# Matrix memory in a two-model transformer kernel: the guard and reciprocal of a token tile's two heads taken in one pass

## The reference

```python
def mlstm_scan(q, k, v, log_i, log_f, state):          # one direction
    ...
        b = jnp.cumsum(fc, axis=-1)
        d_intra = jnp.where(causal, b[..., :, None] - b[..., None, :] + ic[..., None, :], -jnp.inf)
        ...
        w_intra = jnp.exp(d_intra - m_t[..., None])
        s = jnp.einsum('bhtd,bhsd->bhts', qc, kc) * w_intra
        num = w_prev[..., None] * (q C) + jnp.einsum('bhts,bhse->bhte', s, vc)
        qn = w_prev * (q n) + jnp.sum(s, axis=-1)
        h = num / jnp.maximum(jnp.abs(qn), jnp.exp(-m_t))[..., None]

def mlstm_group(...):
    hx_f, hc_f = direction(False, ...)                 # forward
    hx_b, hc_b = direction(True, ...)                  # backward
    y = head_layernorm(hx_f + hx_b, norm_g) * sigmoid(o)
```

## Time and profile before

| | |
|---|---|
| median of 3 runs | 3306.86 us (3305.32 to 3307.8) |
| the profiled execution, own time | 3306.95 us |
| its span | 3305.0 us |
| PE busy | 98% of the span |
| DVE busy | 56% |
| ACT busy | 19% |
| mean granted clock of PE | 0.996 |
| `pairs` of layer 2 | from about 2111.7 to 2325 us |
| `pairs` of layer 3 | from about 2884.6 to 3048 us |

### The profile page before, as it was taken

One profiled execution on the slowest core, in us unless ns is written; L12 is line 12 of the kernel. 1 busy time (PEld: TensorE's weight loads), 2 busy tenths in 40 slices (PEclk: granted clock), 3 DMA queues, 4 the chain that ended last, 5 costly groups with the idle time before them and its releaser, 6 DMA issues.

```text
span 3305.0 us, 40572 instructions
## 1 busy us (share of the span) xinstructions
PE 3224.5 (98%) x15270; PEld 2430.0 (74%) x15270; DVE 1864.2 (56%) x3731; ACT 638.6 (19%) x1339; POOL 160.6 (5%) x307
## 2 busy tenths in 40 slices
PE   7999999999999999999999999999999999999999
PEld 5888865548888878888667886444488887456888
DVE  5887842638887788778353613355274775254100
ACT  2000023421000020000342002355210001254100
POOL 0000000000000000000000100000000000000000
PEclk9999999999999999999999999999999999999999
DMA  7554522114554345544224855211142332331553
GB/s 268 164 175 149 173 70 71 42 49 163 169 169 155 115 153 166 167 153 133 94 80 160 284 155 162 64 52 58 47 158 90 129 120 77 123 101 40 166 152 102
DMA packets 115186, 422.72 MB, mean 128 GB/s; under 512 B 13040, under 2 KB 16368, under 8 KB 112976
## 3 DMA queue, kind: packets, MB, share of 16 engines
q1 hardware_dynamic: 75232, 265.32, 25.0%
q0 software_dynamic: 39504, 154.77, 14.6%
q10 hardware_dynamic: 288, 0.36, 0.0%
HBM read 418.29 MB, written 1.31 MB: 127 GB/s over the span
## 4 chain that ended last, share of the span: by engine, by line
PE 93%; DVE 3%; ACT 2%; issue 1%; DMA 1%; DVEq 0%; ACTq 0%; SPq 0%
PE PS L917 30%; PE PS L969 18%; PE PS L862 11%; PE PS L1423 6%; PE PS L1025 6%; PE PS L1403 3%; PE PS L1347 2%; PE PS L990 2%; PE PS L1265 2%; PE PS L1096 1%; PE PS L1487 1%; PE PS L1203 1%; PE PS L766 1%; PE PS L757 1%; PE PS L1057 1%
## 5 line engine op out<-in xcount | busy, mean ns | idle before, releaser
L862 PE MATMUL PS<-xn,ring 128*128 128x256 f32 (+1 forms) x1504 | 372.0, 408 | 2.8 <-ACT xn L1690 2.3
L862 PEld LDWEIGHTS PS<-xn,ring 128*128 128x128 f32 x1504 | 283.9, 190 | 89.0 <-issue 45.9
L917 PE MATMUL PS<-xn,ring 128*128 128x256 f32 x1312 | 301.4, 383 | 3.7 <-ACT xn L1681 3.7
L917 PEld LDWEIGHTS PS<-xn,ring 128*128 128x128 f32 x1312 | 246.8, 191 | 56.4 <-issue 19.1
L1423 PE MATMUL PS<-xn,arena 128*128 128x512 f32 (+1 forms) x640 | 256.5, 534 | 1.4 <-ACT arena L1913 1.4
L969 PE MATMUL PS<-xn,ring 128*128 128x256 f32 x752 | 223.7, 379 | 0.0
L2202 DVE SCALAR_TENSOR_TENSOR mix<-arena,cond,mix 128x1024 f32<-128x1024 f32 x182 | 222.6, 1278 | 0.0
L969 PE MATMUL PS<-arena,ring 128*128 128x256 f32 x784 | 202.1, 380 | 0.3
L969 PE MATMUL PS<-xn 128*128 128x256 f32 x752 | 193.0, 379 | 0.0
L1025 PE MATMUL PS<-arena,ring 128*128 (+1 forms) x864 | 186.8, 379 | 0.0
L1025 PEld LDWEIGHTS PS<-arena,ring 128*128 128x128 f32 x864 | 164.2, 190 | 22.3
(11 more groups left out here) (327 smaller groups left out, 4892.3 us busy)
## 6 DMA issues: line engine op xcount, KB each, us to landing
ring<-stream SPq DMA_DIRECT2D x500, 512.0 KB, 3.7
arena<-fed_w POOLq DMA_DIRECT2D x200, 512.0 KB, 4.0
arena<-pair_m POOLq DMA_DIRECT2D x8, 1536.0 KB, 7.1
mix<-fed_w POOLq DMA_DIRECT2D x24, 512.0 KB, 3.9
arena<-pair_n POOLq DMA_DIRECT2D x8, 1024.0 KB, 5.4
mix<-gate_sums POOLq DMA_DIRECT2D x32, 256.0 KB, 4.4
mix<-na_bias POOLq DMA_DIRECT2D x8, 512.0 KB, 4.0
h<-xT SPq DMA_DIRECT2D x1, 1024.0 KB, 6.6
```

The costliest lines, as they stand in the source:

```text
L862: m = pe.matmul(PS[:, bank, 0:tokens], ring[:, s, k * P:(k + 1) * P], xn[:, k, 0:tokens], start=k == 0, stop=k == DC - 1)
L917: m = pe.matmul(out, weights, moving, start=k == 0, stop=k == 3)
```

## The change

`weighted(i, n)`, one head of a tile, becomes `weighted(i, t)`, both heads. The four row sums of a tile (two heads by two directions) go to four columns of `small`; maximum, guard and reciprocal are taken once on the four columns instead of twice on two; then come the two scalings of head 0 and the two of head 1. The waits for the weights and scores of head 1 now stand ahead of that one pass. The engines other than DVE are untouched.

```diff
-                def weighted(i, n):
-                    t, e = n // 2, n % 2
-                    w = (wt0, qkn)[e]
-                    dve.wait_ge(pm_w, i * per + (N0 + n + 1))
-                    dve.wait_ge(pm_score, i * per + (N0 + n + 1))
+                def weighted(i, t):
+                    full, less = 1 - t % 2, t % 2
                     spans = (SPAN[t], BOTH[t]) if t % 2 else (BOTH[t], SPAN[t])
-                    for d in range(2):
-                        cols = spans[d]
-                        ins = dve.tensor_tensor_reduce(w[:, d, cols], PS[:, pm_bank(n), cols], w[:, d, cols],
-                                                       1.0, 0.0, ALU.mult, ALU.add, small[:, d:d + 1])
+                    for e in range(2):
+                        n = 2 * t + e
+                        w = (wt0, qkn)[e]
+                        dve.wait_ge(pm_w, i * per + (N0 + n + 1))
+                        dve.wait_ge(pm_score, i * per + (N0 + n + 1))
+                        for d in range(2):
+                            cols = spans[d]
+                            ins = dve.tensor_tensor_reduce(w[:, d, cols], PS[:, pm_bank(n), cols], w[:, d, cols], 1.0,
+                                                           0.0, ALU.mult, ALU.add, small[:, 2 * d + e:2 * d + e + 1])
                     link(ins)
-                    link(stt(small[:, 2:4], small[:, 0:2], -1.0, small[:, 0:2], ALU.mult, ALU.max))
-                    link(tt(small[:, 2:4], small[:, 2:4],
-                            gcol[:, t, 1, :, bass.ds(i * 2 + e, 1)].rearrange("p d o -> p (d o)"), ALU.max))
-                    link(dve.reciprocal(small[:, 4:6], small[:, 2:4]))
-                    if n >= 2:
-                        dve.wait_ge(pm_turned, i * per + (N0 + n - 1))
-                    full, less = 1 - t % 2, t % 2
-                    link(dve.tensor_scalar(probs[:, e, SPAN[t]], w[:, full, SPAN[t]], small[:, 4 + full:5 + full], None,
-                                           ALU.mult))
-                    stt(probs[:, e, BOTH[t]], w[:, less, BOTH[t]], small[:, 4 + less:5 + less], probs[:, e, BOTH[t]],
-                        ALU.mult, ALU.add).then_inc(pm_p, 1)
-                    dve.wait_ge(pm_p, i * per + (N0 + n + 1))
+                    link(stt(small[:, 4:8], small[:, 0:4], -1.0, small[:, 0:4], ALU.mult, ALU.max))
+                    guards = gcol[:, t, 1, :, bass.ds(i * 2, 2)]
+                    lower = small[:, 4:8].rearrange("p (d e) -> p d e", e=2)
+                    link(tt(lower, lower, guards, ALU.max))
+                    link(dve.reciprocal(small[:, 8:12], small[:, 4:8]))
+                    for e in range(2):
+                        n = 2 * t + e
+                        w = (wt0, qkn)[e]
+                        if n >= 2:
+                            dve.wait_ge(pm_turned, i * per + (N0 + n - 1))
+                        scale = lambda d: small[:, 8 + 2 * d + e:9 + 2 * d + e]
+                        link(dve.tensor_scalar(probs[:, e, SPAN[t]], w[:, full, SPAN[t]], scale(full), None, ALU.mult))
+                        stt(probs[:, e, BOTH[t]], w[:, less, BOTH[t]], scale(less), probs[:, e, BOTH[t]],
+                            ALU.mult, ALU.add).then_inc(pm_p, 1)
+                    dve.wait_ge(pm_p, i * per + (N0 + 2 * t + 2))
...
-                    for n in range(per):
-                        weighted(i, n)
+                    for t in range(tiles):
+                        weighted(i, t)
```

More of the change, by code:

```diff
@@ L2706, in pairs @@
                 with dve.Fori(0, HP - 1) as i:
-                    start = loop(i, 7 + 5 * per + tiles)
+                    start = loop(i, 7 + 3 * per + tiles)
                     iteration(i, False)
```

## The result

The changed kernel takes 3369.79 us (median of 4 runs, 3368.08 to 3371.23) against 3307.33 us (4 runs): a ratio of 1.0188, with a 95% interval of 1.0173 to 1.0203. That is 62.5 us slower. The forecast was 3359 us, in a range of 3339 to 3377.

The account below looks back on a forecast made before the run. PE, busy 98% of the span, was taken to bound the kernel. New waits of 38 us plus 14 us of clock gave 52 us on 3306.95, so 3359 us, range 3339 to 3377.

Parts of the forecast that it names:

- Reading where PE waits: PE's waits in L1487 for L2652, 18 times, 18.9 us, are all that a faster DVE could give back.
- What is removed: DVE, 24 tiles of layers 2 and 3: one maximum, guard and reciprocal pass less per tile, 0.71 us each, 17 us.
- Head 0 waits for head 1: Layer 2, tile 0, iterations 2 to 4: head 0's scalings wait for head 1's reductions; PE's first transpose 3.96 us late.
- The chain through ACT in later tiles: Layer 2, tiles 1 to 3: even transposes wait for copy, head 1's weights and DVE; new waits 1.96, 1.07, 1.16 us.
- Sum of the waits: New waits of PE in both layers cost 38 us: 21.7 in layer 2, 16.6 in layer 3.
- The clock: Layers 2 and 3: PE's granted clock falls to 0.50 at long waits, costing 14 us, with 5 and 24 as ends.
- The second: Clock falls after nearly all 16 waits and slow transposes stretch the chain through ACT: above 3374 us; chance 0.1.
- the first: Waits as forecast, but clock falls few or hidden: 38 to 43 us, 3345 to 3350 us; chance 0.2.
- The third: DVE's saving reaches PE: at most all 18.9 us of waits go, 3288, more likely half, 3297 us; chance 0.03.
- The fourth: PE's matmuls cover the later transposes, so no change; chance 0.04.

Follow-up runs that it names:

- the wait alone: Kernel before, steps unmerged, but DVE waits for head 1's weights and scores between head 0's reductions and small steps: 3340.53 us, ratio 1.0102.
- earlier weights: Changed kernel, ACT making head 1's weights for the next iteration's tile 0 before its inverse-sums wait and sigmoid: 3342.15 us, ratio 1.0107.
- run without tile 0: Changed kernel with the merged pass in all tiles but tile 0, which takes its heads one by one as before: 3338.64 us, ratio 1.0092.
- the run with filled waits: Changed kernel with matmuls nobody reads put on PE ahead of each wait for an even transpose: 3345.69 us, ratio 1.0118.
- the run without the guard: Kernel before without L2644, the maximum with exp(-m), so it no longer computes the function: 3300.81 us against 3306.50, ratio 0.9985.
- tile 0 alone: Changed kernel with the merged pass in tile 0 only, other tiles taking heads one by one as before: 3329.19 us, ratio 1.0068.
- the order without the merge: Changed kernel's order, but maximum, guard and reciprocal in two passes of two columns: 3388.62 us, ratio 1.0248.

## Why the prediction was right, point by point

- **Reading where PE waits.** Right: the only line that mattered was L1487 for L2652, and no other line in these stages of the changed trace has new waits.
- **What is removed.** DVE's busy time fell by 13.4 us; 17 was the start-to-start time with its gaps. Four columns cost 0.16, 0.16 and 0.18 us, as taken.
- **Head 0 waits for head 1.** Shown by two runs and the trace: the wait alone costs 34 us, earlier weights give 27.6 back, and DVE's idle 2.76 us for L1988 stands in the rows. The 3.13 us that the forecast put behind the start of head 1 contain the other part, head 1's reductions ahead of head 0's scalings. For T0 3.13 us after the start of head 1 were forecast and 3.15 measured (2185.81 to 2188.96).
- **The chain through ACT in later tiles.** T1 to T2 forecast 6.12, measured 6.19; T3 to T4 5.23 against 5.60, with the clock low around T3; the waits 1.96, 1.07 and 1.16 against 1.90, 1.06 and (T6) 1.02. The run without tile 0 shows it alone.
- **Sum of the waits.** 38 us forecast, 38.5 measured; 24 waits forecast, 24 measured; layer 2 21.7 against 22.5, layer 3 16.6 against 16.0.
- **The clock.** The mechanism was right and the term too small: 14 forecast, 24 measured, both by what is left over and by the run with filled waits. This was the whole of the miss of 10 us. The number of spells was near (11 taken, 13 found); their length was not. I took 1.5 us from the one spell of before, three us long. Four of the 13 lasted 6.8 us, each around and behind a T0, and T0 to T1 lost 2.1 us there. The term's upper end, 24, is where it fell. The row that the term rested on, a fall at the wait of 3.6 us, was a weak one: the same wait brought none in the changed kernel (last section). So that about one spell for each long wait came out right is in part luck.
- **Rivals.** The second, nearly all spells and above 3374, was nearer than the first: 13 of 16 waits brought a spell. The third fell: only in the first iterations were head 1's weights ready in time, and even there the wait ahead of T0 grew, in layer 2 from 1.17 to 2.27 us. That a shorter DVE by itself would give back a part of the old waits is what the run without the guard shows. The fourth, no change, fell too: the waits ahead of T2, T4 and T6 came, where PE's matmuls had covered them.

## What to carry to other kernels

Merging two small steps makes the first of them wait for the inputs of the second. Before counting the saved instructions, look at who makes those inputs and when: here an engine that is 19% busy delivered them 2.8 us too late, in all tiles but the first through a chain that led back to the waiting engine's own last transpose. Where PE is at 98%, give it work that does not depend on the slow chain ahead of its waits; that took a list of numbers and gained 9 us. And count a new PE wait of about two us or more as more than itself: here 38.5 us of waits cost 62.5.

## What the runs showed of the hardware

- PE's granted clock fell to 0.50 not only at waits of 4 to 5 us: in layer 3, directly behind a T2 with a wait of 2.32 us, it was 0.50 from 2937.6 to 2941.0, and in layer 2's first iteration, behind a T2 (2127.90) with a wait of 1.89 us, from 2128.7 to 2132.1. The wait of 2.27 us ahead of the first T0 of layer 2 brought none: T1 followed 2.21 us later, as at full clock. Which one does, these rows do not settle.
- The same wait need not bring the same fall. PE's wait of 3.6 us in L1518 (L1521 where lines moved), at the end of layer 3's stage, is in the traces of all twelve kernels of this document. In six of them the clock then was at 0.50 for 3.4 us, in three for 6.8 us, and in three (the changed kernel, tile 0 alone, the order without the merge) it stayed at 1.00.
- A fall lasted 3.4 us in some stretches and 6.8 in others of the same kernel, so one wait's price is no constant: 0.6 us for each us of new wait in the whole change (24 for 38.5), 0.3 in the run without tile 0 (6.9 for 23.9).
- Idle time filled with useless matmuls made the kernel 24 us faster, with the clock of layer 2's stage at 1.00 instead of 0.94.
- Moving one ACT function past a sigmoid moved a table load of 1.28 us from ACT's idle time into a chain that counted, though no function was added.
